# A hybrid DeltaNet and sliding-window layer on one core: q's first job by quarters, weight remainders at fixed places, first visits joined, output tiles loaded sooner

## The reference

```python
h = einsum('btd,dc->btc', x, w_in)
qa, ka, va, za, ba, aa, qb, kb, vb, zb = split(h)
# A: conv over 4 tokens, silu, l2norm of q and k; then chunks of tokens
a_mat = where(strict, (k_beta @ k.T) * decay, 0)
t_mat = inverse(eye + a_mat)            # triangular
v_new = u - w @ s
o = q_dec @ s + qk @ v_new              # s is the state
s = s * g_tot + k_dec.T @ v_new
ya = rmsnorm(o) * norm_w * silu(za)
# B: window 128, scores with ALiBi, softmax with a sink
yb = (p @ vb) * silu(zb)
y = concat(ya, yb) @ w_out
out = layernorm(2 ** 0.25 * x + y) * ln_g + ln_b
```

## Time and profile before

| | us |
|---|---|
| median of 3 runs | 1141.06 (1137.06 to 1141.7) |
| profiled execution, its own time | 1140.28 |
| span of its trace | 1137.7 |
| PE busy | 1086.6 |
| DVE busy | 727.6 |
| ACT busy | 491.1 |
| POOL busy | 88.7 |

### The profile page before, as it was taken

How to read it: one execution, slowest core, us unless ns; L and a number is a source line. 1 busy time by engine, 2 the same in 40 slices (tenths; PEclk the granted TensorE clock), 3 DMA queues, 4 the chain that set the end, 5 groups by cost and what they waited for, 6 DMA issues and landing times. The chain is left out here.

```text
span 1137.7 us, 18323 instructions
## 1 busy us (share of the span) xinstructions
PE 1086.6 (96%) x6700; PEld 864.6 (76%) x6700; DVE 727.6 (64%) x2123; ACT 491.1 (43%) x1427; POOL 88.7 (8%) x116
## 2 busy tenths in 40 slices
PE   6989989899999999999999999999999999999997
PEld 4867767677878888786887878777787878787785
DVE  5466767677474857657466483866637585857564
ACT  3454646473534344263262534336234545363310
POOL 4300000023300000002000000002000000001240
PEclk9999999999999999999999999999999999999999
DMA  7855575645661724352544362625245343522332
GB/s 261 287 208 192 196 240 183 238 144 185 216 224 50 274 86 174 134 166 86 173 148 162 122 241 84 206 80 199 93 167 187 109 162 121 191 81 66 130 103 82
DMA packets 58120, 183.47 MB, mean 161 GB/s; under 512 B 8432, under 2 KB 21168, under 8 KB 44720
## 3 DMA queue, kind: packets, MB, share of 16 engines
q1 hardware_dynamic: 51376, 173.40, 43.9%
q10 hardware_dynamic: 6656, 8.91, 2.7%
HBM read 138.22 MB, written 44.07 MB: 160 GB/s over the span
## 5 line engine op out<-in xcount | busy, mean ns | idle before, releaser
L782 PE MATMUL bank<-xr,w 128*128 128x512 f32 x2496 | 652.1, 404 | 3.2 <-DVE w L1584 2.1
L782 PEld LDWEIGHTS bank<-xr,w 128*128 128x128 f32 x2496 | 450.4, 189 | 102.3 <-issue 14.4
L833 PE MATMUL bank<-wo,y_split 128*128 128x512 f32 x432 | 114.4, 405 | 0.0
L833 PEld LDWEIGHTS bank<-wo,y_split 128*128 128x128 f32 x432 | 77.4, 188 | 16.1 <-issue 1.0
L1254 ACT ACTIVATE score<-score,neg_max 128x256 f32<-128x256 f32 (+1 forms) x128 | 62.8, 492 | 42.1 <-DVE neg_max L1650 42.1
L1466 DVE SCALAR_TENSOR_TENSOR kq<-conv_in,convw_all,kq 128x512 f32<-128x512 f32 x96 | 73.5, 766 | 2.9
L1802 DVE TENSOR_SCALAR t<-bank,nb_rk 128x128 f32<-128x128 f32 x64 | 22.5, 351 | 73.2 <-PE bank L1034 73.2
L1385 ACT ACTIVATE o_scaled<-bank 128x128 f32<-128x128 f32 x64 | 17.6, 275 | 111.3 <-PE bank L1038 111.1
L1805 DVE SCALAR_TENSOR_TENSOR state<-state,cols_all,bank 128x128 f32<-128x128 f32 x64 | 22.2, 346 | 65.9 <-PE bank L1037 65.7
L1109 ACT ACTIVATE conv_in<-bank 128x512 f32<-128x512 f32 x48 | 28.5, 594 | 75.1 <-PE bank L782 73.3
L1684 DVE TENSOR_TENSOR y_step<-blocks,y_cols 128x60 f32<-128x60 f32 (+14 forms) x240 | 47.9, 200 | 14.1 <-DMA blocks<-n_spill 5.1
(11 more groups left out here) (218 smaller groups left out, 1616.1 us busy)
## 6 DMA issues: line engine op xcount, KB each, us to landing
w<-w_split SPq DMA_DIRECT2D x78, 1024.0 KB, 5.0
w_split<-w SPq DMA_DIRECT2D x26, 1024.0 KB, 4.9
blocks<-n_spill ACTq DMA_DIRECT2D x32, 256.0 KB
y_spill<-y_out SPq DMA_DIRECT2D x30, 256.0 KB, 4.2
y_tile<-w_in SPq DMA_DIRECT2D x13, 512.0 KB, 5.9
x_tile<-w_in SPq DMA_DIRECT2D x13, 512.0 KB, 5.8
y_tile<-y_spill SPq DMA_DIRECT2D x12, 512.0 KB, 6.2
x_tile<-x SPq DMA_DIRECT2D x12, 512.0 KB, 3.8
```

The source lines that it names most:

```text
L782: ins = nc.tensor.matmul(bank[JOBS[at].bank][:], w[:, turn % 3, wp, k, :], xr[:, xp, k], start=(step == 0), stop=(step == 3 * KT - 1))
L833: ins = nc.tensor.matmul(bank[JOBS[at].bank][:], y_place(t)[:, yp, k], wo[:, k, wp, half * UNIT:(half + 1) * UNIT], start=(step == 0), sto ...
```

## The change

The diff does these things:

- At the start the order of loads is x quarter 0, raw tile 0, the other quarters, raw tile 1, w_ba. PE's first job is q, and each of its quarters waits for its own part of x; ba follows. ACT and DVE split in the same order; DVE makes the remainder of turn 0.
- POOL makes turns 1 to 8, and of the later ones those whose job three turns back is a bz (turns 13, 19 and 25), four pieces each. DVE makes the other fifteen, at named points: "bq" ahead of the base inverses, "q" behind them, "k" behind the second half of a convolution and ahead of L1782, "v" behind `divide(n, 1)`, "z" at the slot's end.
- A held rounding is done when the next weight job's result has been copied. At the end of n = -1 the rounding is held too.
- PE's dense steps up to 0.04 are gone: L961 follows L949 at once. In slots 4 to 15 but 12 to 14 the scores and the transposes of v stand together at step 23 (23 / fill). In slots 3, 7, 11 and 15 the turning stands at 0.265.
- `load_y(t)` is called at about 0.05 of the slot (0.16 in slots 4 and 8), and ACT rounds the tile behind 0.35.

```diff
-W_POOL = 7
-        return ["ba", "q", "k", "bT", "v", "kb", "gs", "bz", "gT", "vb", "bq"]
+        return ["q", "ba", "k", "bT", "v", "kb", "gs", "bz", "gT", "vb", "bq"]
...
+def w_by_pool(turn):
+    return 0 < turn < 9 or turn >= 9 and JOBS[W_JOBS[turn - 3]].kind == "bz"
...
-AT_SCORES0, AT_VTOK, AT_TURNS0 = 0.09, 0.15, 0.25
...
+        self.scores0, self.vtok = (0.09, 0.15) if short or n == AH - 1 else (23 / fill, 23 / fill)
+        self.turns0 = 0.265 if long else 0.25
...
             load_x(0, 0)
+            load_raw(0)
+            for k2 in range(1, 4):
+                load_x(0, k2)
+            load_raw(1)
             sp.dma_start(ba_raw[:], w_ba).then_inc(ba_in, 16)
...
+                if t is not None and 0 < i < AH - 1:
+                    load_y(t)
                 if i < AH - 1:
                     after(sp, pt_ready, n, 2)
...
+                if t is not None and i == 0:
+                    load_y(t)
...
                 if t is not None and i < AH - 1:
-                    load_y(t)
                     load_x_tile(t)
...
                 pool.wait_ge(w_high, turn + 1)
+                pool.wait_ge(w_ready, turn)
...
-            for turn in range(W_POOL):
-                w_low(turn)
+            for turn in range(TILES_W):
+                if w_by_pool(turn):
+                    w_low(turn)
...
+                if at == 0 and step % 6 == 0:
+                    x_split(pe, 0, step // 6)
...
-                fill_to(n, AT_KK)
                 after(pe, o_scaled_ready, n - 1, 2)
...
-                fill_to(n, AT_SCORES0)
+                fill_to(n, at.scores0)
                 scores(n, 0)
-                fill_to(n, AT_VTOK)
+                fill_to(n, at.vtok)
...
-                fill_to(n, AT_TURNS0)
+                fill_to(n, at.turns0)
...
                 if at in W_AT and W_AT[at] + 3 < TILES_W:
-                    if at + 1 < len(JOBS) and JOBS[at + 1].n > max(job.n, -1) >= 0:
+                    split_weight()
+                    if JOBS[at + 1].n > job.n:
                         held.append(W_AT[at] + 3)
...
                 load_blocks(n)
-                split_weight()
                 after_jobs(n, 0.18)
...
-                after_jobs(n, 0.4)
                 if t is not None and i < AH - 1:
                     round_y(t)
...
+            def weight_rest(n, kind):
+                turn = W_AT[JOB_AT[kind, n if kind == "z" else n + 1]] + 3
+                if turn < TILES_W and not w_by_pool(turn):
+                    w_low(turn)
...
                 convs(n, 0.2)
+                if n < AH:
+                    weight_rest(n - 1, "bq")
                 after_jobs(n, at.base)
-                w_lows(n, 0.3)
...
                 base_inverses(n)
                 if t is not None and i < AH - 1:
                     split_y(t)
+                if n < AH - 1:
+                    weight_rest(n, "q")
                 gate_b(n, 0)
...
                 convs(n, 0.34, 1)
-                w_lows(n, at.p16)
...
                 convs(n, 0.34, 1)
+                if n < AH - 1:
+                    weight_rest(n, "k")
                 after(dve, inv_done, n, 4)
...
-                w_lows(n, at.p32)
+                if n < AH - 1:
+                    weight_rest(n, "v")
...
                     after_jobs(n, at.chunk(c, 0.8))
-                    w_lows(n, at.chunk(c, 0.67))
...
                 after_jobs(n, 1)
-                w_lows(n, 1)
+                if n < AH - 1:
+                    weight_rest(n, "z")
```

More of the change, by code:

```diff
@@ L169, in x_landing @@
     return ((0, 2 * u - 1), (1, u + 1), (4, u - 1), (0, 2 * u))[k2]
-AT_KK = 0.04
-AT_SCORES0, AT_VTOK, AT_TURNS0 = 0.09, 0.15, 0.25
 class Places:
@@ L1234, in _ @@
             x_hi(0, 0)
-            x_hi(0, 1)
             w_hi(0)
-            x_hi(0, 2)
-            x_hi(0, 3)
+            for k2 in range(1, 4):
+                x_hi(0, k2)
             w_hi(1)
@@ L1407, in x_low, with w_low @@
                     .then_inc(x_low_dve, 1)
+            def w_low(turn):
+                flat = lambda part: w[:, turn % 3, part].rearrange("p k n -> p (k n)")
+                dve.wait_ge(w_high, turn + 1)
+                if turn > 0:
+                    dve.wait_ge(w_ready, turn)
+                nc.vector.tensor_tensor(flat(1), raw_stage[turn % 2][:], flat(0), ALU.subtract).then_inc(w_ready, 1)
+            def weight_rest(n, kind):
+                turn = W_AT[JOB_AT[kind, n if kind == "z" else n + 1]] + 3
+                if turn < TILES_W and not w_by_pool(turn):
+                    w_low(turn)
             nc.vector.memset(ones[:], 1.0)
@@ L1417, in _ @@
             nc.vector.memset(lower32[:], 0).then_inc(tail_put.sem, 1)
+            x_low(0, 0)
+            w_low(0)
+            for k2 in range(1, 4):
+                x_low(0, k2)
             dve.wait_ge(ba_in, 16)
@@ L1421, in _ @@
             nc.vector.tensor_tensor(ba_w[:, :, 1], ba_raw[:], ba_w[:, :, 0], ALU.subtract).then_inc(setup, 1)
-            for k2 in range(4):
-                x_low(0, k2)
             dve.wait_ge(const_in, 144)
@@ L1572, in after_jobs @@
                 normalise(n, f)
[L1574 to L1585, removed]
             beta_place = [0]
@@ L1618, in _ @@
             after_jobs(-1, 1)
-            w_lows(-1, 1)
             def gate_a(n):
```

## The result

| | before | changed |
|---|---|---|
| median, us | 1141.16 (5 runs) | 1148.93 (5 runs, 1146.95 to 1154.29) |
| profiled execution, its own time | 1140.28 | 1148.24 |
| span | 1137.7 | 1145.4 |
| mean granted clock of TensorE | 0.998 | 0.994 |

The ratio is 1.0075, with a 95% interval of 1.0053 to 1.0098: some 8 us slower, 1.9 us beyond the upper end of the forecast range.

A forecast was written before the change was run, and what follows sets the result against it. PE was taken as busy nearly throughout, so only its 42.7 us of idle time could be won or lost. Terms from the start (-1.4) through the slots summed to +0.3, giving a forecast of 1141 us, range 1133.5 to 1147.

The forecast's parts named there:

- Remainder of q behind the base inverses: Slots 0 to 2: PE waits for q's remainder made after the inverse; L986 comes 1.5 to 1.6 us later per slot.
- Remainder of k: Slots 0 to 2: k's remainder directly ahead of transpose L1782 delays PE's L1008, +1.2 us in each slot.
- bz's remainder by POOL: State chunks of slots 0 to 2: PE's wait of 1.36 for a residual goes, -1.4 us each.
- Joined visit, the cover: L961 waits for o_scaled at 11 slot boundaries, together 6.8 us; much is paid back within the slots, some 2 remain.
- not paid back: Rival, joined visit: all 6.8 us of waits for o_scaled remain instead of some 2, giving 1146 us; chance 0.1.
- Joined visit, the scores: Scores move from step 18 to 23, so the inverse ends later: +0.7 us at L986 in slots 5, 6, 9 and 10.
- three jobs of slack: nothing: Slots 4 and 8: SyncE queue stands some 4 us for a spill ahead of the next weight load, at no cost.
- Start: Before slot 0: q ahead of ba lets PE start at about 9.8; gain 1.4 us, between 0.3 and 2.
- Slot 0, its first third: Held rounding starts ACT's chain 2.9 us earlier; PE's waits of 1.17 and 2.38 fall to some 0.7; 2.5 to set against.
- Output tiles sooner: Loads some 10 us sooner remove PE's waits at L991: slot 10 -0.9, slot 6 -0.7, slot 8 -0.5, slot 4 +0.5 us.
- Moved remainders do not hold PE: Faster rival, slots 0 to 2: q and k remainders are done before PE needs them, 1133 us; chance 0.24.
- ACT held by a late raw tile: Slower rival, slots 0 to 2: ACT's tile wait delays the copy for L1003 by 1.9 us each, 1146.7 us; chance 0.12.

The follow-up runs named there:

- second run: The changed kernel as it is, run again beside the kernel before on another chip: 1149.13 us, ratio 1.0083 of the kernel before.
- q late alone: Kernel with both remainders, scores, value transposes and cover at their old places, but q's remainder again behind the base inverses: 1138.34 us, ratio 0.9973 of before.
- The experiment with PE kept busy: Changed kernel plus 12 unused matmuls ahead of PE's wait for bz's weight in slots 1 and 2: 1146.29 us, ratio 1.0054 of before.
- the better base: Changed kernel with both remainders (q, k), scores, value transposes and the 0.04 cover at their old places: 1129.73 us, ratio 0.9906 of before.
- the scores late alone: Kernel with both remainders, scores, value transposes and cover at old places, but scores and value transposes joined at step 23: 1134.9 us, ratio 0.9942 of before.

## Why the prediction was wrong

The mechanisms stood nearly as forecast; their sizes did not. Summed by part, the forecast had 13.2 us of cost (the table above) and 12.9 of gain. Measured were 18.6 (uncertain by some 11) and about 10.7 (the ratio 0.9906, uncertain by 2.6). By these figures the miss of 7 to 8 is 5.4 of cost too little and 2.2 of gain too much; that split is an estimate.

- **Remainder of q behind the base inverses.** Sized at 1.6 us a slot. The wait was as predicted, 3.08 and 3.09 us at L794 in slots 1 and 2 released by the remainder (3.07 to 4.28 in the second run), 2.03 in slot 0, and no wait at L997 there. The failed term is its price: 7.6 instead of 4.8. I priced a wait by its length alone; 1.7 us of half clock behind each of two waits, 3.4 in all, is more than the difference of 2.8, and over all executions q late alone lost 3 to 4 us more by the clock than its base. Rows for it were scarce in the trace of before, where the clock stayed at 1.00 behind 2.38 us. The experiment with PE kept busy shows that the half clock in slots 1 and 2 belongs to these waits.
- **Remainder of k.** 1.2 in each slot was forecast, 0.9 seen at L1019, and 3.2 measured for 3.6. Right on this base, within 3 us; alone on the changed kernel it gave nothing back, which stays open.
- **bz's remainder by POOL.** -4.2 forecast, -4.4 measured, within 3; the 1.36 waits are gone. Right. The loss on DVE by POOL's work, kept as an upper bound of 2, was not seen here but was there as soon as POOL worked beside instructions with two SBUF inputs.
- **Joined visit, the cover.** Waits for o_scaled add up to 5.1, the longest 1.52 at slot 11 and 1.48 at slot 7, against 6.8 and 1.7 forecast (the recorded rows give 1.62 at slot 7). The doubtful step is "much of it is paid back inside the slot": 3.7 remained on the better base and about 5 on the changed kernel, not 2. Each is uncertain by 3, so this step is likely wrong and not shown to be. The rival "not paid back", with a chance of 0.1, has the whole 6.8.
- **Joined visit, the scores.** 2.8 forecast (0.7 in four slots), 4.1 measured. Waits at L997 came, 0.33 in slot 5 and 0.73 in slot 9, none in 6 and 10, so not for the whole amount. A second way has no term in the prediction: its "three jobs of slack: nothing" is about a spill in slots 4 and 8, not about a weight load that stands behind the scores. In slot 6 SP issued the next weight load 1.4 us later in the slot than before, behind the decay load that follows the scores:

```profile
446.41 0.32 SPq L571 DMA_DIRECT2D decay<-g_rows  x1
446.82 0.39 SPq L544 DMA_DIRECT2D w<-w_split  x1
```

  and PE then waited 1.83 for the tile at 457.64, for 5.7 us in all slots where before had 0.5. How much of it belongs to the change is not settled: slot 6's 1.83 came again in the second run of the same kernel, but its total was 3.0, the variants had between 0.5 and 5.9, and with the scores late alone it was 1.0, too little for that part's 4.1.
- **Start.** PE began at 9.25 (forecast 9.8), and slot 0 came 2.6 sooner (1.4 forecast); 1.8 by the run with the old start, not clear of none. In the second run slot 0 came 1.5 sooner. The two differ in how long the slow pace lasted, for which I put 5 us: q's 24 steps took 7.18 in the first (all at 0.24 would take 5.8, so by estimate some 3 us were slow) and 8.53 in the second, and k began at 20.06 and 21.34 (forecast 21.3, before 22.72).
- **Slot 0, its first third.** 2.5 of gain, and 0.9 in slot 1, were set against the later remainder. The failed step is "PE's waits for it fall to some 0.7": the 1.17 at the scores went, but PE still waited 2.40 at L919 (1.31 in the second run). L919 came 15.4 us into the slot where L907 had come at 16.6, so 1.2 of the 2.5 were won in this trace. I let ACT begin the chain some 2.9 us earlier relative to PE; it began 2.8 us into the slot, where it had been 4.4. ACT was not waiting there: its table load of 1.28 us began 1.0 into the slot (0.1 before), and q's copy came behind it. What the put-off rounding is worth is the rest of 10.7 less 1.8, 4.4 and 4.3, that is 0.2 where I had 3.4; that rest carries the errors of all four and holds the other small moves (the turning at 0.265, z's place) too, and no run tried the rounding alone.
- **Output tiles sooner.** Some 3.9 of gross gain forecast, 4.3 measured (uncertain by 3 to 4). A wait of 0.9 in slot 8 remained at L1002, where I wanted none over 0.5.
- **The rivals.** "Moved remainders do not hold PE" fell: the waits are there. "ACT held by a late raw tile" fell too: in slots 0 to 2 no wait for ACT stands ahead of L1014. The change as a whole fell on the side to which I gave 0.16.

What stays open: which of the shorter waits bring the half clock. It came with 17 of 19 waits of 3 us or more, with one of 2.40 and not with one of 2.38, and with about half of those of 1.7 behind the inverse. The two profiles of the changed kernel differ too: one has three such stretches, at 70 to 75, 142 to 146 and 200 to 204, the other none at 70, one at 83 to 87, one of double length at 141 to 149, begun while PE still stood, and one at 203 to 207.

## What to carry to other kernels

Where PE is 95% busy, a wait of 3 us costs more than 3 us: price it with the half-clock stretch that followed 17 of 19 such waits here and made it half as long again, and do not take a wait of 1.7 to be free of it. Work that keeps PE moving meanwhile, even useless work, kept the clock up. A remainder or any other producer belongs ahead of a long serial chain on its engine if its consumer comes first in the other engine's order; saving the chain 1.2 us a slot cost 2.5 a slot here (7.6 over three slots). And a change of many parts is best read by putting each part into the best base alone: here four parts lost some 19 us and hid the 11 that the others won.

## What the runs showed of the hardware that was not expected

A wait of 3.08 us in an otherwise full kernel was followed, 1.4 us after work began again, by some 3.4 us at half granted clock (0.54, 0.50, 0.50, 0.75 in four windows of 1 us). Such a stretch came with 17 of 19 waits of 3.07 us or more, 22 of 53 between 1.6 and 2.4, and none of 84 between 1.2 and 1.6, and each took 1.7 us of clock, or twice that. With PE at work for 2.88 of that wait the clock stayed at 1.00. Each of POOL's pieces of 0.7 us stopped one DVE instruction of 0.21 with two SBUF inputs, which then took 0.66 to 0.79.
